# Giving up 1,152 free bytes of SBUF in a two-layer decoder kernel: the split x, the constants and the region of h move down

## The reference, cut to what matters

```
for l in range(DEPTH):
    proj = x @ w_in[l]
    ...
    mixed = jnp.concatenate([attn, conv], axis=-1) @ w_out[l]
    x = layer_norm(DEEPNORM_ALPHA * x + mixed, ln1_g[l], ln1_b[l])
    ffn = peer_ffn(x, peer_wq[l], peer_keys[l], peer_u[l], peer_v[l])
    x = layer_norm(DEEPNORM_ALPHA * x + ffn, ln2_g[l], ln2_b[l])
```

## Time and profile before

| | |
|---|---|
| median of three runs | 1840.21 us (1838.8 to 1842.12) |
| the profiled execution: its own time | 1838.61 us |
| its span, first to last instruction | 1836.8 us |
| granted TensorE clock, mean | 0.999 |
| PE busy | 1822.5 us (99%) |
| DVE, ACT, POOL busy | 78%, 53%, 16% |

### The profile page before, as it was taken

The page is one execution under the profiler, slowest core; times in us unless marked ns, Lnnn a source line. Parts: engine busy times, 40 slices in busy tenths (PEclk is TensorE's granted clock), DMA queues, the critical chain, the costliest instruction groups (busy, mean ns, idle before and its releaser), DMA issues.

```text
span 1836.8 us, 36357 instructions
## 1 busy us (share of the span) xinstructions
PE 1822.5 (99%) x11904; PEld 1557.2 (85%) x11904; DVE 1429.6 (78%) x2576; ACT 966.3 (53%) x1597; POOL 302.5 (16%) x269
## 2 busy tenths in 40 slices
PE   9999999999999999999999999999999999999998
PEld 8789988888888888888887898888888888888887
DVE  8869999788888888444498699997888788874445
ACT  4655565555554444555546555655555544445554
POOL 0000000000003333455400000000000033335553
PEclk9999999999999999999999999999999999999999
DMA  8444656555555555766574456565555555557663
GB/s 258 153 160 162 198 181 198 177 173 166 176 172 173 172 172 181 248 192 192 169 216 137 160 171 200 182 200 165 183 167 171 165 183 177 174 183 239 192 191 123
DMA packets 95965, 333.06 MB, mean 181 GB/s; under 512 B 11680, under 2 KB 16032, under 8 KB 95648
## 3 DMA queue, kind: packets, MB, share of 16 engines
q1 hardware_dynamic: 88992, 317.51, 53.3%
q10 hardware_dynamic: 6912, 14.77, 2.5%
HBM read 328.20 MB, written 4.03 MB: 181 GB/s over the span
## 4 chain that ended last, share of the span: by engine, by line
PE 94%; DVE 3%; DMA 1%; issue 1%; ACT 1%; ACTq 0%; DVEq 0%; SPq 0%
PE bank L1682 24%; PE bank L1431 15%; PE bank L1433 14%; PE bank L1432 14%; PE bank L1681 11%; PE bank L1702 3%; PE bank L1387 2%; PE bank L1389 2%; PE bank L1388 2%; PE bank L1684 1%; PE bank L1503 1%; DVE top_index_u L1085 1%; DVE lo L811 1%; PE bank L1649 1%; DMA shifted_u<-x_kept 0%
## 5 line engine op out<-in xcount | busy, mean ns | idle before, releaser
L811 DVE TENSOR_TENSOR lo<-raw,hi 128x1024 fp32r<-128x1024 f32 x600 | 753.5, 1257 | 224.6 <-ACT hi L467 223.2
L467 ACT ACTIVATE hi<-raw 128x1024 fp32r<-128x1024 f32 x600 | 633.1, 1057 | 428.3 <-PE bank L1433 374.9
L1682 PE MATMUL bank<-xt,hi 128*128 128x512 f32 x1920 | 662.6, 397 | 0.0
L445 POOL TENSOR_TENSOR w_split<-h,w_split 128x256 fp32r<-128x256 f32 x256 | 300.3, 1174 | 1517.3 <-ACT w_split L747 1103.5
L1681 PE MATMUL bank<-xt,lo 128*128 128x256 f32 x1680 | 468.2, 279 | 0.0
L1431 PE MATMUL bank<-hi,w_split 128*128 128x512 f32 x1024 | 402.1, 393 | 0.0
L1682 PEld LDWEIGHTS bank<-xt,hi 128*128 128x128 f32 x1920 | 345.6, 188 | 64.1
L1433 PE MATMUL bank<-hi,w_split 128*128 128x512 f32 x1024 | 398.9, 390 | 0.0
L1432 PE MATMUL bank<-lo,w_split 128*128 128x512 f32 x1024 | 398.3, 389 | 0.0
L1681 PEld LDWEIGHTS bank<-xt,lo 128*128 128x128 f32 x1680 | 316.5, 188 | 10.9
L707 ACT ACTIVATE h<-bank 128x256 f32 (+1 forms) x240 | 92.3, 384 | 305.1 <-PE bank L1682 305.1
(11 more groups left out here) (199 smaller groups left out, 1690.8 us busy)
## 6 DMA issues: line engine op xcount, KB each, us to landing
raw<-in_stream SPq DMA_DIRECT2D x600, 512.0 KB, 3.9
shifted_u<-x_kept ACTq DMA_DIRECT2D x16, 142.0 KB, 4.6
ln_g<-in_ln_p ACTq DMA_DIRECT2D x4, 512.0 KB, 6.1
ln_b<-in_ln_p ACTq DMA_DIRECT2D x4, 512.0 KB, 7.9
keys_sb<-in_keys_t ACTq DMA_DIRECT2D x2, 1024.0 KB, 5.0
x_kept<-x ACTq DMA_DIRECT2D x4, 512.0 KB, 4.6
x<-x_kept ACTq DMA_DIRECT2D x4, 512.0 KB, 5.3
shifted_u<-x_kept ACTq DMA_DIRECT2D x8, 130.0 KB, 4.1
```

The costliest lines, as they stand in the source:

```text
L445: nc.gpsimd.tensor_tensor(ws[:, j, 1, :], h[:, ds(i * (RING * SEQ) + j * SEQ, SEQ)], ws[:, j, 0, :].bitcast(f32), ALU.subtract).then_inc(* ...
L467: nc.scalar.activation(hi[:, j, :], raw[:, j, :], ACT.Copy).then_inc(*hi_done.one)
L811: vec.tensor_tensor(lo[:, j, :], raw[:, j, :], hi[:, j, :].bitcast(f32), ALU.subtract).then_inc(*lo_done[j].one)
L1682: last = mm(dst[:, :], w_hi, both, start=k == 0, stop=k == KC - 1)
```

## The change

The line that leaves 1,152 bytes free is taken out:

```diff
         key_block = place("key_blocks", [P, 5, SEG], f16)
         gate_part = place("gate_part", [P, GROUPS, PARTS, GROUP, 2], f16)
 
-        used[0] += 1152
+
         xt_at = used[0]
         xt = place("xt", [P, KC, 2, SEQ], f32r)
         ws = place("w_split", [P, RING, 2, SEQ], f32r, at=xt_at)
```

## The result

The changed kernel takes 1857.64 us (median of six runs, 1857.27 to 1858.71) against 1840.22 us: a ratio of 1.0098 with a 95% interval of 1.0087 to 1.0109, 17.4 us slower. The forecast was no change, with a range up to 1845.6 us; it missed.

A forecast was written before the change was run, and what follows sets the result against it. PE's matmul rate was taken as the bound; all address terms cost 0, so the profiled 1838.6 us stays, given as the runs' median, 1840.2 us. Range 1836.4 to 1845.6 us for 8 in 10.

The forecast's parts named there:

- What bounds the kernel: Whole kernel: PE busy 1822.5 of 1836.8 us at full clock, so the rate of matmuls, read from distances of starts, decides.
- PE's busy time moves by over 3.7 us: Whole kernel: the stated sign that the prediction of no change is wrong; 3.7 us is about 0.2%.
- the first of the four kinds of access: u and v stages: PE's reads of xt and w_split, whose start goes from remainder 128 by 256 to 0; cost 0.
- the gate tables: Gate stretch: one-hot table pairs at remainders 128 and 0 take PE 194 and 193 ns, taken as evidence for cost 0.
- The even starts of the v stage: v stage: 13 starts 226 ns apart, no irregular one, taken as a sign against colliding reads of PE.
- The bound named for this case: v stage: upper bound if every product became as slow as the u stage's look, 8 ns x 3072 = 24.6 us.
- Rival A: u stage: PE's two readers collide by address, 120 tiles get 0.04 us each, + 4.8 us, 1845.0 us; chance 0.13.
- The uneven tiles: u stage: neighbouring tiles take 2.82 and 2.78 us in turn, read as a possible sign of an address collision.
- rival C: Stretch of the choice: DVE's work on h slows, deciding from 9%; at 15% + 7.8 us, 1848.0 us; chance 0.04.
- rival D: DMA transfers into h cost more; PE's 1.0 us wait doubled gives + 1.0 us, 1841.2 us; chance 0.02.

The follow-up runs named there:

- d = 64: xt and w_split placed 64 bytes lower than in the kernel before the change, h stays; 1847.62 us in one run.

## Why the prediction was wrong

**What bounds the kernel** was read rightly: PE alone, and there the distance of starts. The end moved by as much as PE's busy time, and no new wait came. "PE's busy time moves by over 3.7 us" was the stated sign of being wrong; it moved by 19.2.

**The step that failed** is the first of the four kinds of access, "PE's reads of xt and w_split ... I cost this at 0". It was taken from the earlier trace rows: the gate tables at remainder 128 and at remainder 0 take 194 and 193 ns on PE. But in both places `onehots` stands 3,072 bytes behind `gated`, twelve times 256. The pair varies the own address and holds the difference between weights and moving operand fixed, and the difference is what counts. The pair was also compared by durations, which the prediction itself had set aside ("distances of starts do"); the distances, 29.9 and 29.2 ns before, are 29.8 and 29.2 in the changed kernel. After the change the rows were as flat as before (groups of the changed kernel, 352 to 548 us), while the v stage lost 5.8 ns:

```profile
L1253 DVE TENSOR_TENSOR onehots_2u<-key_blocks,i_t 128x1536 f16<-128x1536 f16 x15 | 14.3, 951 | 0.0
...
L1264 DVE TENSOR_TENSOR gated_2u<-onehots_2u,gate_part 128x1024 f16<-128x1024 f16 x15 | 10.3, 686 | 0.0
L1702 PE MATMUL bank<-gated_2u,onehots_2u 128*128 128x64 f16 x240 | 9.5, 193 | 0.5 <-DVE gated_2u L1264 0.5
```

That the trace shows slots and blocks at steps of whole KB was true and answered nothing about a shift with another remainder by 256.

**The even starts of the v stage** were read as a sign against a collision. They were the sign that this stage had the difference 0, the best of those tried, and therefore everything to lose. The bound named for this case, 8 ns x 3072 = 24.6 us, was of the right term and the right order: 5.8 ns x 3072 = 17.8 us, of which 16.1 are found by adding up. That it came close is luck in part, since its 8 ns are a difference of durations in the u and the v stage (397 and 389 ns), not of distances. It was kept out of the range.

**Rival A** named the mechanism, two reads of PE, and priced it in the wrong stage: 4.8 us in the u stage, where the mean of a tile stayed at 2.80 us. The second of its signs, "uneven starts in the v stage", did come: 227 to 242 ns where there had been 226 and 227. The uneven tiles that made me look there depend on something else. Kernels with unchanged remainders (all up by 128; `xt` down by 256 or by 1,024) have 666.6 us in the wide u tiles too, not 664.3, so the 2.3 us between the two traces are not the remainder's, and their cause stays open. Each kernel has one trace, and the times of one kernel lie up to 5.4 us apart (1837.75 to 1843.16 with all up by 128), so it may be the execution and not the layout.

**The Trainium skill**, "TensorE: Matmul & The Clock Gate" ("Step-by-step: what each phase is for"), says that loading the next weights takes nothing from the running matmul. The v stage shows a case in which the two reads do get in each other's way, by 5.8 ns on 226.6, and the measurement decides.

**DVE, ACT, POOL, rival C**: rightly put at nothing. ("ACT less everywhere" is not so in the v stage, where ACT is busy for 77.54 us and DVE for 70.85; nothing hung on it.) Line 818 in the stretch from 200 to 330 us of the changed kernel, beside 423 ns in the earlier trace rows:

```profile
L818 DVE TENSOR_TENSOR h<-bank,h 128x256 f32<-128x256 f32 x46 | 19.7, 428 | 0.0
```

1% and not the 9% that it takes, and the run that moved `h` alone measured no change.

**DMA, rival D**: the wait of line 1503 went from 1.0 to 1.2 us; moving `h` alone cost nothing. What the Trainium skill says in "DMA: Bandwidth & Descriptors" ("How a descriptor splits into AXI transactions") could be true and is not felt here.

## What to carry to other kernels

Where PE is the bound, note for each stage the start addresses of what gives the weights and of what streams, and keep their difference at a multiple of 256 bytes until a run shows something better; a tensor inserted or taken out in between changes it. In the v stage both tensors are read in pieces that start at multiples of 512 bytes, so the tensors' starts tell the difference. The runs show this for 512 columns in float32, weights changed each time, and for no other shape. Two placements of a pair in which both tensors move together say nothing about a move of one of them. When every engine but one is quiet and a change touches that one's operands, the bound computed for that engine belongs into the range, not only beside it.

## What was not expected of the hardware

The distance of two 512-column float32 products whose weights change each time depends on the difference of the two tensors' addresses, taken by 256 bytes: 226.6 ns at 0, 229.1 ns at 64 bytes lower, 232.4 at 128, 233.5 at 32, 192 and 224. Moving both leaves it (1839.36 us), moving either one by 128 bytes costs 17.2 and 18.5 us (1856.22 against 1839.07 us, 1857.87 against 1839.38 us). For products with 256 columns the order was another: the narrow products of the projections (lines 1387 to 1389) have a mean distance between starts, of those under 150 ns over the whole trace, of 120.0 ns before, 118.8 ns in the changed kernel, and 115.1 ns with d = 64. One execution of each was traced. Why 32 bytes cost more than 64, why all three products slow down when only `lo` moves, and what in PE's two reads meets, no run here tells.
